# Attention scores with a 64-row pair of matmuls in place of two full ones

## The reference

```python
def attend(qblk):
    sc = jnp.einsum('bqkgd,bskd->bkgqs', qblk, k).astype(jnp.float32) * scale
    p = jax.nn.softmax(sc, axis=-1).astype(v.dtype)
    return jnp.einsum('bkgqs,bskd->bqkgd', p, v)
```

## Time and profile before

| | |
|---|---|
| median of 3 runs | 2303.51 us (2303.42 to 2306.13) |
| the profiled execution's own time | 2303.42 us |
| its span, first to last instruction | 2301.7 us |
| TensorE busy | 2267.3 us, 99% |
| VectorE busy | 1077.5 us, 47% |
| ScalarE busy | 888.7 us, 39% |
| attention loops | about 272 to 478 us and 832 to 1038 us of the span |

### The profile page before, as it was taken

How to read it: one execution, slowest core, us unless ns; L and a number is a source line. 1 busy time by engine, 2 the same in 40 slices (tenths; PEclk the granted TensorE clock), 3 DMA queues, 4 the chain that set the end, 5 groups by cost and what they waited for, 6 DMA issues and landing times.

```text
span 2301.7 us, 28551 instructions
## 1 busy us (share of the span) xinstructions
PE 2267.3 (99%) x11640; PEld 1919.2 (83%) x11640; DVE 1077.5 (47%) x1439; ACT 888.7 (39%) x1426; POOL 274.1 (12%) x276
## 2 busy tenths in 40 slices
PE   8999999999999999999999999999999999999998
PEld 7887799988888779998788898887888888888887
DVE  4313399954433259983624252335334344342343
ACT  5222477744322257773434152323222222222232
POOL 0097200000029600000013020000000000000000
PEclk9999999999999999999999999999999999999999
DMA  6111000043311000003421101222111111124232
GB/s 202 37 55 37 1 1 1 1 138 116 90 53 56 19 1 1 1 9 121 147 60 37 64 19 37 100 94 90 39 55 55 36 55 50 41 101 146 92 128 73
DMA packets 104210, 141.48 MB, mean 61 GB/s; under 512 B 11670, under 2 KB 65094, under 8 KB 104102
## 3 DMA queue, kind: packets, MB, share of 16 engines
q1 hardware_dynamic: 104102, 139.97, 18.4%
HBM read 123.18 MB, written 16.78 MB: 61 GB/s over the span
## 4 chain that ended last, share of the span: by engine, by line
PE 95%; DVE 3%; ACT 1%; issue 1%; DMA 0%; DVEq 0%; SPq 0%; ACTq 0%
PE ps L199 24%; PE ps L201 24%; PE ps L200 24%; PE ps L983 5%; PE ps L998 3%; PE ps L999 3%; PE ps L970 2%; PE ps L971 2%; PE ps L947 1%; PE ps L275 1%; PE ps L228 1%; PE ps L934 1%; PE ps L1962 1%; PE ps L684 1%; PE ps L1971 1%
## 5 line engine op out<-in xcount | busy, mean ns | idle before, releaser
L199 PE MATMUL ps<-w_hi,hT_hi 128*128 128x512 f32 (+1 forms) x1760 | 678.5, 386 | 2.4 <-DVE hT_lo L238 1.4
L201 PE MATMUL ps<-w_hi,hT_lo 128*128 128x512 f32 (+1 forms) x1760 | 671.9, 382 | 0.0
L200 PE MATMUL ps<-w_lo,hT_hi 128*128 128x512 f32 (+1 forms) x1760 | 671.5, 382 | 0.0
L183 DVE TENSOR_TENSOR w_lo<-w_raw,w_hi 128x2048 fp32r<-128x2048 f32 x89 | 207.7, 2334 | 539.9 <-ACT w_hi L167 537.3
L199 PEld LDWEIGHTS ps<-w_hi,hT_hi 128*128 128x128 f32 x1760 | 331.2, 188 | 66.9 <-issue 2.1
L201 PEld LDWEIGHTS ps<-w_hi,hT_lo 128*128 128x128 f32 x1760 | 331.0, 188 | 64.5
L200 PEld LDWEIGHTS ps<-w_lo,hT_hi 128*128 128x128 f32 x1760 | 331.4, 188 | 62.5 <-issue 0.5
L167 ACT ACTIVATE w_hi<-w_raw 128x2048 fp32r<-128x2048 f32 x71 | 135.9, 1914 | 504.4 <-PE ps L201 504.4
L199 PE MATMUL ps<-hT_hi,w_hi 128*128 128x512 f32 x832 | 324.1, 390 | 2.1 <-DVE hT_lo L290 1.7
L201 PE MATMUL ps<-hT_hi,w_lo 128*128 128x512 f32 x832 | 323.7, 389 | 0.0
L200 PE MATMUL ps<-hT_lo,w_hi 128*128 128x512 f32 x832 | 323.7, 389 | 0.0
(11 more groups left out here) (203 smaller groups left out, 2363.9 us busy)
## 6 DMA issues: line engine op xcount, KB each, us to landing
w_raw<-in_ffn_w_up SPq DMA_DIRECT2D x44, 512.0 KB, 5.0
w_raw<-in_ffn_w_down SPq DMA_DIRECT2D x22, 1024.0 KB, 5.0
w_raw<-in_w_in SPq DMA_DIRECT2D x21, 1024.0 KB, 5.1
x_mid<-X SPq DMA_DIRECT2D x24, 512.0 KB, 2.9
w_raw<-in_gla_w_in SPq DMA_DIRECT2D x12, 1024.0 KB, 5.2
X<-in_x SPq DMA_DIRECT2D x16, 512.0 KB, 7.0
w_raw<-in_w_out SPq DMA_DIRECT2D x8, 1024.0 KB, 6.7
X<-x_mid SPq DMA_DIRECT2D x16, 512.0 KB, 7.5
```

The source lines that it names most:

```text
L183: engine.tensor_tensor(self.p.w_lo[:, slot, 0:size], self.p.w_raw[:, slot, 0:size], plane(self.p.w_hi[:, slot, 0:size]), ALU.subtract).the ...
L199: nc.tensor.matmul(out, a_hi, b_hi, start=first, stop=False)
L200: nc.tensor.matmul(out, a_hi, b_lo, start=False, stop=False)
L201: return nc.tensor.matmul(out, a_lo, b_hi, start=False, stop=last)
```

## The change

Per tile the two full matmuls with the low queries go. Two matmuls with 64 rows each take their place, at the head of the tile's scores: the low queries times the high keys of the first half on partitions 0 to 63, and the same for the second half on partitions 64 to 127. The two full matmuls with the high queries follow and end both banks. The product low x low is no longer computed.

For the second matmul of the pair the high keys of the second half must stay on partitions 64 to 127. The scratch of the setup becomes `KT_up`, which keeps them for both key heads in the same 4 KB that `KT_hi` had. The first half's scratch goes to a part of `QT_hi` that is not yet in use at that time. The instructions and semaphores of the setup are otherwise the same.

```diff
-        self.KT_hi = prog.at("KT_hi", [P, SEQ], kb + 88, F32R)
+        self.KT_up = prog.at("KT_up", [P, KV, SEQ // 2], kb + 88, F32R)
...
+    def low_keys(self, i):
+
+        return self.KT_up[HD:P, i // 2, :] if i % 2 else self.QT_hi[HD:P, 1, 0:SEQ // 2]
...
                 self.gates(pe, 2 * n + 2)
+            g, tok = head // (H_B // KV), slice(t * P, (t + 1) * P)
+            nc.tensor.matmul(prog.ps[:, 2 * (n % 2), :], self.QT_lo[0:HD, head % 2, tok],
+                             self.KT_st[0:HD, g, 0:512], start=True, stop=False)
+            nc.tensor.matmul(prog.ps[:, 2 * (n % 2) + 1, :], self.QT_lo[HD:P, head % 2, tok],
+                             self.KT_up[HD:P, g, :], start=True, stop=False)
             for half in range(2):
-                keys = self.KT_st[:, head // (H_B // KV), half * 512:(half + 1) * 512]
-                out = prog.ps[:, 2 * (n % 2) + half, :]
-                nc.tensor.matmul(out, self.QT_hi[:, head % 2, t * P:(t + 1) * P], keys, start=True, stop=False)
-                mm = nc.tensor.matmul(out, self.QT_lo[:, head % 2, t * P:(t + 1) * P], keys, start=False, stop=True)
+                mm = nc.tensor.matmul(prog.ps[:, 2 * (n % 2) + half, :], self.QT_hi[:, head % 2, tok],
+                                      self.KT_st[:, g, half * 512:(half + 1) * 512], start=False, stop=True)
             mm.then_inc(self.s_ready, 1)
...
-            nc.scalar.activation(self.KT_hi[HD:P, cols], prog.ps[HD:P, self.turn_bank(i), :], ACT.Copy
+            nc.scalar.activation(self.low_keys(i), prog.ps[HD:P, self.turn_bank(i), :], ACT.Copy
...
-                                    plane(self.KT_hi[HD:P, i % 2 * 512:(i % 2 + 1) * 512]), ALU.subtract
+                                    plane(self.low_keys(i)), ALU.subtract
```

## The result

| | before | changed |
|---|---|---|
| median, 6 runs each | 2305.46 us | 2321.14 us |
| range | 2303.42 to 2306.13 | 2319.09 to 2322.94 |
| span of the profiled execution | 2301.7 us | 2318.8 us |
| VectorE's wait for scores, whole run | 51.3 us | 62.3 us |

The changed kernel is slower: ratio 1.0069, 95% interval 1.0056 to 1.0082, or 15.7 us by the medians. The two profiled spans differ by 17.1 us. The forecast was slower, 2330.4 us (+26.9), with 2284 to 2352 for the range.

The account below looks back on a forecast made before the run. The prediction took TensorE's stream in the attention loops as the bound. Per tile -0.23 + 0.19 + 0.19 + 0.06 = +0.21 us, x128 = +26.9 us on 2303.5, gave 2330.4 us, range 2284 to 2352.

Parts of the forecast that it names:

- The bound: In the attention loops the time is the sum of what TensorE streams, 3.15 us a tile, while VectorE keeps up.
- The gain of 0.23 us a tile: In the scores, two full matmuls go (-0.46 us) and two parallel 64-row ones come (0.23 us).
- Going in, 0.19 us: Change from 128 to 64 rows ahead of the pair: its load waits for the full matmul, 0.19 us a tile.
- Coming out, the same 0.19 us: Change from 64 back to 128 rows behind the pair, taken to cost as much as going in, 0.19 us.
- rivals A and B: Changes of rows: A, no waiting, about 2283 us, chance 0.24; B, only one direction costs, +3 us, chance 0.12.
- The second half, 0.06 us: In the pair, the second 64-row matmul's load can't hide under an earlier matmul and starts 0.06 us after the first.
- VectorE and ScalarE, which wait for scores already, only wait longer: In the loop, the whole added 0.21 us a tile lies on TensorE's chain; the other two engines just wait longer.
- Four of the signs: Expected in the timeline: full load 0.3 us after second half, pair to transposes 0.95, period 3.36, VectorE's wait +0.2 a tile.
- The case's own range: The main case's whole-kernel time, from moving its sum 0.1 us a tile each way: about 2317 to 2345 us.

Follow-up runs that it names:

- e3: The changed kernel with both 64-row matmuls of the pair on the same rows, 0 to 63; 2348.04 us.
- e4: The changed kernel with the pair taken apart per tile: 64-row half, full half, 64-row half, full half; 2396.45 us, 1.0406 of before.
- e2: The changed kernel with the pair replaced by two 96-row low-query matmuls, so part of low x low comes back; 2305.68 us, 1.0001 of before.
- e5: The kernel before, with the output's turning (four small matmuls) moved behind the values' matmuls of its iteration; 2299.01 us, 0.9973 of before.
- e8: The changed kernel with the pairs of two tiles together behind the transposes, and VectorE's maximum of even tiles behind its subtractions; 2406.53 us.

## Why the prediction was right, and where its terms were off

- **The bound** held but for 24 places (below). Before and after, the loop is TensorE's stream; the page, the chain and VectorE's longer wait for scores (51.3 to 62.3 us) agree.
- **The gain of 0.23 us a tile** held: e3 takes the parallelism away, and the trace shows 0.23 us more.
- **Going in, 0.19 us**, from one 44-row sample, held. The pair's load starts 0.21 us after the value matmul, 0.09 us past the slot at 0.12 us, and 0.10 us of it is exposed. e4 shows the same with full matmuls ahead.
- **Coming out, the same 0.19 us**, an assumption for which no row existed, held as well (e4: 0.42 us against 0.23 us). This is what rules out rivals A and B. The Trainium skill ("TensorEngine Tiling (Array Packing)", Key Properties) says that changing the tiling mode drains TensorE; the late loads of this trace agree with it in both directions.
- **The second half, 0.06 us, was mis-sized: 0.01 us.** I had taken the spacing of the four 44-row loads, which all go to the same rows. The loads of the pair, to different rows, start together. The Trainium skill's figure of about 4 ns apart ("TensorE: Matmul & The Clock Gate", Part 3) fits what the trace can resolve. With the measured 0.01 us the sum is 0.16 us a tile; the trace has 1.21 - 1.04 = 0.17 us, 128 x 0.17 = 21.8 us.
- **"VectorE and ScalarE, which wait for scores already, only wait longer" was wrong.** TensorE had a wait of its own on VectorE that I passed over, since the chain counted it to L947: 0.63 us instead of 0.39 us in 24 iterations. Longer scores fill 0.16 us of it each, 3.8 us. 21.8 - 3.8 = 18.0 us, against 17.1 us between the spans and 15.7 us between the medians. The timelines settle most of the rest. From a layer's first transposes of probabilities to its last it is 471.70 - 276.53 = 195.17 and 1031.70 - 836.55 = 195.15 us before, 481.23 - 278.24 = 202.99 and 1048.84 - 846.26 = 202.58 us in the changed kernel: 15.3 us more in both together. Of the other 1.8 us between the spans 1.4 lie ahead of the first scores (271.88 against 273.29 us), and they aren't the change's: e2, as fast as before, starts its scores at 273.10 us.
- **Four of the signs** were off. The load of the first full matmul starts 0.42 us after the pair's second half, where the prediction wrote 0.3: it had counted the exposed 0.10 us of the pair's own load in its sum but not in this sign. For the same reason its 0.95 us from the pair's start to the transposes doesn't fit its own sum, which gives 1.25 - 0.21 = 1.04 us; measured were 320.42 - 319.42 = 1.00 us. The tile's period is (329.12 - 302.98) / 8 = 3.27 us instead of 3.36, and VectorE's wait for scores grew by 11.0 / 128 = 0.09 us a tile instead of 0.2 (0.11 with the 3.5 us ahead of the maximum that the view charges elsewhere: 51.3 us idle in all before, 65.8 after). Both are smaller for the reasons of the last two points. The case's own range was rounded up as well: 128 x 0.1 = 12.8 us each way is 2317.6 to 2343.2 us.

So of the 26.9 us forecast 128 x 0.05 = 6.4 were the second half and 3.8 the wait. Both errors went the same way, so none hid the other; the mechanism and the sign were right.

The best version found leaves the pair out: e5, the kernel before with the output's turning behind the values, at 2299.01 us, beats before (0.9973) and the changed kernel.

## What to carry to other kernels

Count both changes of rows before splitting the array: here they cost 0.19 us each, 0.38 us together, and two 512-column matmuls side by side save 0.23 us, so nothing is won unless about two such pairs run in one stay. With two the trace shows 0.03 us won per two tiles, and only where the banks were free in time. In a stream where loads hide under matmuls, look at when a load starts, not only at what a matmul lasts: one sample of a late load gave this price. Compare the duration of the same short group of matmuls in different iterations; where one is longer (0.63 against 0.39 us), a wait may be hidden in the stream. Here moving other work ahead of it gained 6.2 us.

## What the runs showed of the hardware that I had not expected

- 96-row matmuls between full ones cost nothing that the time shows (e2, 256 of them, 2305.68 against 2305.52 us); 64-row ones in the same places (e3) cost 0.38 us for each stay, that is for going from 128 rows to 64 and back.
- Directly behind the four small matmuls of an output a change of rows cost 0.04 us less than behind the values (3.32 against 3.36 us an iteration).
- In e8, where TensorE was busy 136.2 of 160 us between 280 and 440 us, the granted clock of that stretch was 0.93, against 1.00 in the same stretch of before. Part of its 101 us is that. As an estimate from the mean granted clocks of the two executions (0.984 and 0.999), at most 0.015 x 2405 = 36 us; how much of that counts wasn't tried.
